# Two-layer hybrid encoder step on one core: delta rule and input parts earlier among the attention tasks, output tiles spread over the last tasks, a place of its own for the third output unit

## The reference, cut to what matters

```python
hn = rmsnorm(x) ; parts = split_columns(hn @ w_in)        # one input projection, 23 units of 128 columns
A = gated delta rule over chunks of 64 tokens, 4 heads    # prompt: 8 chunks in sequence, sample: 1
B = sliding-window attention with sinks ; C = latent attention ; D = short gated convolution
x = x + concat([A, B, C, D]) @ w_out                      # output projection, 8 units of 128 columns
x = x + square(relu(rmsnorm(x) @ w1)) @ w2
x = x + (p[l] @ w_ple) * sigmoid(rmsnorm(x) @ w_gate)
```

## Time and profile before

| what | value |
|---|---|
| median of 3 runs | 1614.86 us (1613.15 to 1617.97) |
| the profiled execution's own time | 1612.89 us |
| its span in the trace | 1611.1 us |
| TensorE busy | 1525.2 us, 95% |
| VectorE, ScalarE, GpSimd busy | 1050.8, 670.0, 832.0 us |
| mean granted clock of TensorE | 0.988 |

### The profile page before, as it was taken

One profiled execution on the slowest core, in us unless ns is written; L12 is line 12 of the kernel. 1 busy time (PEld: TensorE's weight loads), 2 busy tenths in 40 slices (PEclk: granted clock), 3 DMA queues, 4 the chain that ended last, 5 costly groups with the idle time before them and its releaser, 6 DMA issues.

```text
span 1611.1 us, 33871 instructions
## 1 busy us (share of the span) xinstructions
PE 1525.2 (95%) x14198; PEld 1439.6 (89%) x14198; DVE 1050.8 (65%) x1754; ACT 670.0 (42%) x1186; POOL 832.0 (52%) x467
## 2 busy tenths in 40 slices
PE   6999999899999999998999999998999999999896
PEld 6889787799999999988998897878999999999895
DVE  6865557656848567596677645664487584756954
ACT  6521433335544343453455223342454443434522
POOL 3344111165766849486543431112759486684943
PEclk9999999999999999999999999999999999999998
DMA  5211001152241414213322110113333224141221
GB/s 197 79 41 42 27 28 40 46 133 92 79 132 53 132 53 118 80 53 100 104 67 67 41 39 17 41 40 73 113 97 96 89 79 132 53 133 51 66 80 69
DMA packets 43960, 123.81 MB, mean 77 GB/s; under 512 B 10976, under 2 KB 13792, under 8 KB 43552
## 3 DMA queue, kind: packets, MB, share of 16 engines
q1 hardware_dynamic: 43664, 119.86, 24.1%
q10 hardware_dynamic: 144, 1.78, 0.3%
HBM read 117.86 MB, written 3.76 MB: 75 GB/s over the span
## 4 chain that ended last, share of the span: by engine, by line
PE 73%; DVE 18%; issue 3%; ACT 3%; POOL 1%; DMA 0%; SPq 0%; POOLq 0%; DVEq 0%; ACTq 0%
PE psum_p L1736 37%; PE psum_t L1777 16%; PE psum_p L1791 5%; PE psum_t L1827 5%; DVE conv_out L1277 2%; DVE hidden L1241 2%; PE psum_p L1970 1%; PE psum_p L1950 1%; PE psum_p L1756 1%; PE psum_t L1943 1%; PE psum_t L1938 1%; POOL w_rest L779 1%; DVE probs L1491 1%; DVE x L1588 1%; DVE mla_q L1308 1%
## 5 line engine op out<-in xcount | busy, mean ns | idle before, releaser
L1736 PE MATMUL psum_p<-hidden,w_high 128*128 128x272 f32 x3776 | 637.6, 291 | 10.9 <-POOL w_rest L779 8.6
L1736 PEld LDWEIGHTS psum_p<-hidden,w_high 128*128 128x128 f32 x3776 | 537.0, 189 | 15.6 <-POOL w_rest L779 10.3
L779 POOL TENSOR_TENSOR w_rest<-raw,w_high 128x1024 fp32r<-128x1024 f32 x114 | 280.5, 2464 | 464.9 <-ACT w_high L899 464.9
L1736 PE MATMUL psum_p<-hidden,w_rest 128*128 128x272 f32 x1888 | 391.2, 289 | 0.0
L1736 PEld LDWEIGHTS psum_p<-hidden,w_rest 128*128 128x128 f32 x1888 | 296.9, 189 | 0.0
L791 POOL TENSOR_TENSOR w_rest<-w_sums,w_high 128x512 fp32r<-128x512 f32 x128 | 207.7, 1648 | 93.3 <-DVE w_sums L1533 55.3
L899 ACT ACTIVATE w_high<-raw 128x1024 fp32r<-128x1024 f32 x114 | 120.1, 1055 | 192.4 <-PE psum_p L1736 115.4
L1777 PE MATMUL psum_t<-hidden_split_a,w_high 128*128 128x272 f32 x896 | 178.5, 290 | 12.8 <-issue 7.7
L1777 PE MATMUL psum_t<-hidden_split_b,w_high 128*128 128x272 f32 x896 | 177.1, 288 | 0.4 <-DVE hidden_split_b L1549 0.4
L1777 PEld LDWEIGHTS psum_t<-hidden_split_a,w_high 128*128 128x128 f32 x896 | 140.0, 188 | 17.3 <-issue 17.1
L1777 PEld LDWEIGHTS psum_t<-hidden_split_b,w_high 128*128 128x128 f32 x896 | 140.3, 188 | 0.8 <-DVE hidden_split_b L1549 0.8
(11 more groups left out here) (289 smaller groups left out, 2578.0 us busy)
## 6 DMA issues: line engine op xcount, KB each, us to landing
raw<-w_units SPq DMA_DIRECT2D x146, 512.0 KB, 3.6
raw_more<-w_units SPq DMA_DIRECT2D x64, 512.0 KB, 3.6
x<-x_t SPq DMA_DIRECT2D x8, 272.0 KB, 6.3
y_t<-y SPq DMA_DIRECT2D x8, 272.0 KB, 2.1
constants<-consts ACTq DMA_DIRECT2D x1, 1737.5 KB, 8.1
ple_in<-p_t SPq DMA_DIRECT2D x2, 544.0 KB, 11.0
constants<-consts SPq DMA_DIRECT2D x1, 1088.0 KB, 5.3
w_kv<-w_kv SPq DMA_DIRECT2D x2, 256.0 KB, 5.2
```

Of the source, the lines that this page charges most:

```text
L779: mark(pool.tensor_tensor(wlo_at(l, s, 2), raw_at(l, u), whi_at(l, s, 2).bitcast(F32), ALU.subtract), lo_done)
L1736: ins = pe.matmul(pp[:, 2 * b + h, 0:HALF], w(l, s, 2)[:, cols(k)], rhs[:, k, part, h * HALF:(h + 1) * HALF], start=(n == 0 and z == 0), s ...
```

## The change

1. `CHAIN_IT` becomes 26, so the chain's parts are spread over steps 0 to 25, and everything in `late` that is counted from it comes five steps earlier. The last gated split comes at step 33 and not at 38.
2. The input parts are spread over 33 steps (`PART_IT`), so the last one is at step 32 and not at 37.
3. The output tiles (6, 7, 4, 5), which were one part, are two. Parts 0 to 2 of output unit 0 come at steps 34 to 36, those of unit 1 at 38 to 40, and the last parts of both at 41.
4. The third output unit (`U_OUT + 2`) has a place of its own, `RING`, in the memory of `mla_q`. ScalarE makes its high part at `("out", 1, 0)`, after the last scores, and no longer after output unit 0. Output unit 4 follows unit 0 in its place.
5. On SP's queue eight stores are issued before the loads of the last two input units, two loads (output units 3 and 4) come before the wait for the last tail, and only the two stores of the short convolution wait for it.

```diff
@@ place_of, unit_follows
+    if u == U_OUT + 2:
+        return RING
...
+    if u == U_OUT + 4:
+        return l, U_OUT
@@ schedule
-CHAIN_IT = N_TASKS - 7
-OUT_TILES = ((2, 3), (0, 1), (6, 7, 4, 5))
+CHAIN_IT = N_TASKS - 12
+PART_IT = N_TASKS - 5
+OUT_TILES = ((2, 3), (0, 1), (6, 7), (4, 5))
...
-            CHAIN_IT + 6: [("gated", 1, 1)], N_TASKS: [("gated", 1, 2), ("out", 0, 0)], N_TASKS + 1: [("out", 0, 1)], N_TASKS + 2: [("out", 1, 0)],
-            N_TASKS + 3: [("out", 1, 1), ("out", 0, 2), ("out", 1, 2)]}
+            CHAIN_IT + 6: [("gated", 1, 1)], CHAIN_IT + 7: [("gated", 1, 2)],
+            PART_IT + 1: [("out", 0, 0)], PART_IT + 2: [("out", 0, 1)], PART_IT + 3: [("out", 0, 2)],
+            N_TASKS: [("out", 1, 0)], N_TASKS + 1: [("out", 1, 1)], N_TASKS + 2: [("out", 1, 2)],
+            N_TASKS + 3: [("out", 0, 3), ("out", 1, 3)]}
...
-        while q < len(parts) and q < (it + 1) * len(parts) // N_TASKS:
+        while q < len(parts) and q < (it + 1) * len(parts) // PART_IT:
@@ memory
+        whi_more.append(place("w_high_third", [P, D], F32R, at=qc_at)[0])
+        wlo_more.append(place("w_rest_third", [P, D], F32R, at=qc_at + 4 * D)[0])
@@ sync
-                for u in range(3, U_OUT + 4):
-                    load_unit(l, u)
-                wait_apart(sp, roped.at(l, 5), v_raw.at(l, 1), c_done.at(l, 1), mixed_d.at(l, 2))
+                for u in range(3, N_IN - 2):
+                    load_unit(l, u)
+                wait_apart(sp, roped.at(l, 5), v_raw.at(l, 1), c_done.at(l, 1))
...
+                for u in range(N_IN - 2, U_OUT + 3):
+                    load_unit(l, u)
                 sp.wait_ge(*s_dve.at(l, NCH))
...
+                load_unit(l, U_OUT + 3)
+                load_unit(l, U_OUT + 4)
+                sp.wait_ge(*mixed_d.at(l, 2))
...
-                load_unit(l, U_OUT + 4)
@@ scalar
+                if u == U_OUT + 2:
+                    act.wait_ge(*score.at(l, N_TASKS))
+                elif unit_follows(l, u) is not None:
...
+                    elif item == "out" and (n, p[0]) == (1, 0):
+                        high(l, U_OUT + 2)
...
-                    high(l, U_OUT + SPLIT + m)
+                    if m:
+                        high(l, U_OUT + SPLIT + m)
```

More of the change, by code:

```diff
@@ L434, in build @@
         assert 4 * 28 * HALF + 4 * D <= 4 * KT * 2 * TOK and 4 * D <= 8 * (SEQ + 6 + DEC) and 8 * D + 32 <= 16 * TOK
+        whi_more.append(place("w_high_third", [P, D], F32R, at=qc_at)[0])
+        wlo_more.append(place("w_rest_third", [P, D], F32R, at=qc_at + 4 * D)[0])
+        assert 8 * D <= 16 * TOK
         hq, _ = place("hidden_parts", [P, 8, HALF], at=prob_at)
@@ L895, in high @@
                 wait_raw(act, l, u)
-                if unit_follows(l, u) is not None:
+                if u == U_OUT + 2:
+                    act.wait_ge(*score.at(l, N_TASKS))
+                elif unit_follows(l, u) is not None:
                     k, o = unit_follows(l, u)
@@ L1813, in out_part @@
                                             start=(part == 0 and k == tiles[0] and z == 0),
-                                            stop=(part == 2 and k == tiles[-1] and z == 2))
-                if part == 2:
+                                            stop=(part == 3 and k == tiles[-1] and z == 2))
+                if part == 3:
                     mark(ins, proj)
```

## The result

| | before | after |
|---|---|---|
| median, first comparison | 1613.80 us (1611.09 to 1617.97, 6 runs) | 1605.43 us (1604.22 to 1606.72, 6 runs) |
| median, second comparison, at another time | 1613.73 us (1607.33 to 1618.61, 17 runs) | 1607.71 us (1603.40 to 1609.41, 12 runs) |
| the profiled execution, its span | 1612.89 us, 1611.1 us | 1606.72 us, 1604.9 us |

The ratio is 0.9944 (95% interval 0.9932 to 0.9957) in the first and 0.9960 (0.9948 to 0.9973) in the second. The change is worth 6 to 8 us; I had forecast no change, 1614.6 us.

What follows compares the result with a forecast made beforehand. TensorE works 1525.2 of the 1611.1 us span, so only its idle time or clock could change. Per layer 9.9 us added against 9.5 removed gives 1613.7; plus 2.0 to the median, less 1.1, 1614.6 us; range 1607.5 to 1619.5.

Steps and rivals of the forecast that it cites:

- The low clock: Behind the new stop before the turn of task 32, TensorE's clock falls again, costing the same 1.6 us per layer.
- TensorE's busy time: Over the kernel, expected as before apart from the clock, since the change removes or adds no matmul.
- The pile-up: VectorE's tails and gates packed beside 512-key prompt tasks, around step 33, make TensorE wait for copies: 5.6 us per layer.
- the chain's copy: At step 25, two chain parts back to back; the copy between them queues behind ScalarE's weight high part: 1.2 us.
- the drain's 0.7: At the drain, nothing is left between the last values and the tiles needing them: 0.7 us, split 0.5 and two latencies.
- the head's 0.5: At chain steps 0 and 1, only one task's scores cover VectorE's work behind the state product: 0.5 us wait.
- The lock: GpSimd's low parts hold VectorE's chain right-hand sides in blocks 3 and 7: 1.7 us per layer, bounds 0 and 4.4.
- The 1.1 us that I took off: Correction for both layers: the same count on the old order gave 9.2 us of waits where the trace has 8.4.
- What goes: TensorE's existing waits in the tasks and output projection, all 9.5 us per layer, go at their present places.
- rival (c): The third output unit's place gives nothing, raw weights or score wait being late: 0.7 us per layer back, 1616; chance 0.05.
- The base: Step from the profiled execution to the median of the runs shown: 2.0 us added, 1613.7 to 1615.7.
- Rival (a): Smaller VectorE pile-up at step 33: stop at most 1 us, clock stays up, 7.4 us less, about 1607.2; chance 0.22.

Runs made afterwards that it cites:

- experiment 6: Kernel after plus two useless VectorE products ahead of each layer's last gated split, to lengthen the stop; 1611.87 us, ratio 0.9982 to the kernel before.
- experiment 8: Kernel after plus two useless VectorE products ahead of each layer's last inverse level, to move the stop later; 1608.65 us, ratio 0.9964 to the kernel before.
- experiment 1: Kernel before plus only the third output unit's own place, with the fifth unit following the first; 1612.24 us, ratio 0.9978 to the kernel before.
- experiment 3: Kernel before with only the new order of SyncE's (SP's) queue; 1615.28 us, ratio 0.9996 to the kernel before.
- experiment 7: Kernel before plus the third output unit's place and the new SyncE queue order, old order of tasks, chain and tiles; 1608.76 us, ratio 0.9970.
- experiment 2: Kernel after without the third output unit's own place, new queue order kept; 1613.52 us, ratio 0.9992 to the kernel before.
- experiment 9: Kernel after with only the chain spread over one task step more, last tail left in step 33; 1600.85 us, ratio 0.9926 to the kernel before.
- experiment 4: Kernel after with VectorE's last tail moved from step 33 to step 34; 1600.85 us, ratio 0.9908 to the kernel before.
- experiment 5: Kernel after with the chain one task step longer and no tail in step 33; 1595.41 us, ratio 0.9883 to the kernel before.

## Why the prediction was wrong, step by step

The forecast rested on this sum: 9.9 us added against 9.5 removed per layer and the low clock unchanged, so +0.4 us per layer. The stretch that holds all these steps became 4.0 us shorter. The 4.4 us between are three steps that failed, of nearly the same size: the low clock 1.5 us, TensorE's busy time 1.5 and the waits 1.3, with 0.1 in gaps too small for the list.

- **The low clock.** "I expect the low clock again, behind turn 32, at the same 1.6 us": the size was right (1.53 by experiments 6 and 8; the rows it was read from give 1.8, since three tiles of 0.75 and a turn of 0.34 are 2.6 us and not 2.8), but it did not come, in either layer of either trace.
- **What the runs showed in its place.** All ten stops of 2.73 us in the old order (both traces of before, experiments 1, 3 and 7, each in both layers) were followed by the low clock, and so were both of 4.48 us. Of the stops in the new order, those of 2.95 us were not in four of four cases in the kernel after, were in two of two in experiment 8, in one of two without the third place (2); the two of 2.60 us both were (9). The measure that I used, idle time within a few microseconds, does not order these cases: 2.60 us fell, 2.95 did not. Neither does the time from the trace's start: the stage begins anywhere from 182.85 to 185.65 us in the thirteen traces, and 1.8 us apart in experiments 4 and 5 (184.84 and 183.07), which are the same up to there.
  What does order them stands in the traces' records of the granted clock. The falls of one trace lie on a grid: the distances between their beginnings are whole multiples of one step, to 0.01 us, in all thirteen traces (in the kernel before they begin at 27.72, 311.03, 737.70, 785.48, 819.62, 1102.92 and 1529.59 us). So it can be told where the next point of the grid lay behind a stop at which no fall began:

| stops | length (us) | next grid point behind the stop's end (us) | low clock |
|---|---|---|---|
| old order, ten | 2.73, 2.74 | 0.37 to 1.48 | all ten |
| experiment 6 | 4.48, 4.48 | -0.11, 0.27 | both |
| experiment 8 | 2.96, 2.95 | 1.03, 1.05 | both |
| experiment 9 | 2.60, 2.60 | 0.55, 1.05 | both |
| experiment 2 | 2.96, 2.96 | 0.88, 1.91 | the first |
| after, two traces | 2.95, 2.95, 2.94, 2.95 | 1.79, 1.84, 1.63, 1.55 | none |

  The side branch's first stop, 2.92 to 2.99 us in every kernel and in code that no edit touches, is a second set of 26, and it goes the same way: the 17 with a point from 0.86 us ahead of the stop's end to 1.50 behind it fell, the nine whose next point lay 1.77 to 2.35 us behind it did not. In the kernel after both stops simply lay too far ahead of a point. This was read from the traces afterwards; no experiment set the distance on purpose. In the two traces of the kernel after the first falls begin at 28.00 and 27.79 us, so the grid lay nearly the same in both; that the clock stayed up twice in both layers is therefore luck of the place and may differ in other executions.
  The Trainium skill (TensorE: Matmul & The Clock Gate, Part 1, "The HAM clock gate") says that the chip judges the engine's activity in windows that run freely and do not start with the kernel. The traces agree: the grid lies differently against the kernel's start from trace to trace.
- **TensorE's busy time** was put at "as before, apart from the clock", with the whole effect to come "from TensorE's idle time, or from its clock". By the windows it fell from 217.14 to 214.15 us per layer, 1.5 of it beside the fall (0.5 with place and queue, 0.95 with the order, experiments 7 and 8), for the same 1900 matmuls. No term of the sum had it. Pairs of score matmuls of 384 keys, for one, took 0.91 us in the kernel before and take 0.81 in the kernel after. It is no surcharge on every wait: where waits for copies changed alone (4, 5, 6, 9), the stretch moved by their listed time or up to 0.2 us less. Its cause stays open.
- **The pile-up was right**, but for one of its turns: 3.1 us before turn 32 was 2.95; 1.0 before turn 31 was 1.18; 1.2 at turn 29 was 1.05; 0.3 at turn 28 was 0.89 (at 291.10 and 286.16 us); the chain's copy 1.2 was 0.99; the drain's 0.7 was 0.58; the head's 0.5 was 0.36. Experiment 4 showed by taking the tail away that the cause is the one named.
- **The lock was mis-sized**: 1.7 us per layer in the sum, at most 0.55 in the trace (waits of 0.31 at 214.46 and 0.25 at 258.44 us). VectorE's timeline of block 3:

```profile
210.91 0.29 DVE L1477 TENSOR_TENSOR chain_r<-psum_t,decay_columns 128x128 f32<-128x128 f32 x1
211.23 1.90 DVE L1478 TENSOR_TENSOR chain_r<-v_beta,chain_r 128x128 f32<-128x128 f32 x1
```

  and GpSimd's low part beside it, with that of block 7:

```profile
210.61 2.38 POOL L790 TENSOR_TENSOR w_rest<-raw,w_high 128x1024 fp32r<-128x1024 f32 x1 [11.20 <-ACT w_high L912]
...
252.05 2.42 POOL L790 TENSOR_TENSOR w_rest<-raw,w_high 128x1024 fp32r<-128x1024 f32 x1 [11.09 <-ACT w_high L912]
```

  In block 3 the second operation was caught until GpSimd's had ended (212.99), 1.6 us more than its usual 0.29. The 0.31 us wait stands behind it in all eight traces that have this order of the chain, and in none of the five with the old one. In block 7 VectorE's operation began at 251.93, 0.12 us ahead of GpSimd's, took 0.29 and cost nothing. The mechanism was right for this pair (The Trainium skill, SBUF — State Buffer, "Who interferes with whom", says the same of two SBUF inputs, and the trace agrees with it here); the row that the prediction put under that rule, the scaling at 305.19, has one tensor and one column of 32 rows as inputs and not two tensors, so it is no example of the rule in the words used there, though its 2.17 us show that it was held. I had priced one catch in the middle of the chain at nearly its full length, when most of it was covered. No experiment took the lock away by itself.
- **The waits in sum** were 8.6 us and not 9.9, 1.3 us per layer, of which the lock is 1.1. The 1.1 us that I took off for both layers for having counted too high was less than half of this.
- **What goes** was right: all waits of before at their places went, the GpSimd waits of the third and fifth unit among them. But 0.66 us was too little for what the place is worth in the new order: without it 2.13 us come back (2). The price of rival (c) was read from a row of the old order, where a longer drain hid most of it. In the trace after, the fifth unit's high part waits for TensorE and no more for its transfer, which answers to the earlier trace rows:

```profile
1122.33 1.06 ACT L912 ACTIVATE w_high<-raw 128x1024 fp32r<-128x1024 f32 x1 [4.03 <-PE psum_p L1752]
```

- **What is given back** was not foreseen either: 2.8 us at the layers' ends, where the clock no longer falls in covered time but behind the second stop. In layer 0 it is in both traces of the kernel after (the second stop's wait is 2.84 and 2.85 us) and in neither of before (1.40 and 1.35). It is no effect of the work changed, but of where the stops come to lie: experiments 1 and 3, of the old order, have it in layer 1 (2.86 us), and experiments 4 and 8, of the new order, have it in neither (1.30 to 1.35).
- **The base.** I added 2.0 us to go from the profiled execution of before to the median. The median of after lies 1.3 us below its profiled execution in the first comparison and 0.6 below in the second. This step, 3.3 us of the 9.2 between 1614.6 and 1605.4, was chance in the choice of traces.

The 9.2 us add up so: clock 3.1, busy time with the small gaps 3.1, waits 2.6 less the 1.1 taken off, base 3.3, less 1.8 for what lies outside the stretches (given back 2.8, 0.8 between the layers, 0.2 elsewhere).

Rival (a) named the outcome (1607.2 us, "the clock stays up") but tied it to a stop of at most 1 us. The stop was 2.95 us and the clock stayed up all the same, so that its number came near is luck. The range, which began at 1607.5, did not even hold it; it should have let the clock stay up by itself, on top of a count of waits that might be 1 us per layer too high.

## What to carry to other kernels

A hand count of what stands ahead of one reduction on VectorE, from rows of the same shapes, gave six of seven new waits to 0.25 us, and the same count found the better orders of experiments 4 and 5 (at best 4.4 us less in each layer's stretch, 218.4 against 222.8). When several edits meet at one place (a shorter drain, and a place that makes its next unit ready), price each in the new order and not by its row in the old one. Where a stop is long enough for the clock to fall at all, give the fall a chance and not a certainty, let the range hold both, and look whether TensorE has time to spare behind it. Compare two kernels at the same number of falls before giving a difference to an edit: so taken, the new order gave 0.1 to 0.2 us per layer here, and place and queue 2.3.

## What the runs showed of the hardware

- The low clock comes in falls of one size, 1.7 us of TensorE's work (in five traces also two in a row), of which 1.53 us reach the end where TensorE sets it, and nothing where it would wait anyhow (the first stop of the side branch in the kernel before). The thirteen traces have three to eight of them ahead of the last 20 us. Within a trace they begin on one grid, to 0.01 us. The kernel before varies from 1607.33 to 1618.61 us in one comparison, and its two traces differ by one fall in number and in three places.
- Behind the same stop of 2.95 us, with the same work around it, the granted clock was 1.00 in the kernel after (both layers, two traces) and 0.61 to 0.62 in experiment 8 (both layers); in a third (2) the two layers differed. Of 48 stops of 2.6 to 4.5 us, the 34 with a grid point from 0.9 us ahead of their end to 1.5 behind it had the low clock at their end or behind it; the 14 whose points lay 1.06 us or more ahead and 1.55 or more behind had not.
- A VectorE product of 0.29 us took 1.90 beside GpSimd's subtraction of 2.38 us, in both layers of all eight traces with this order of the chain (after twice, 2, 4, 5, 6, 8 and 9), with a wait of TensorE of 0.3 us behind it.
